# Mixer's first phase in a new order of copies, and weight splits placed anew at stage borders, in a two-block fp32 layer

## The chip, the cores and the metric
One core of a Trainium2 chip. The metric is the device time of one execution in microseconds (us), the median of several. Five engines share an on-chip memory (SBUF) and the accumulator banks (PSUM, eight banks `PS[0..7]` of 128 partitions by 2 KB): TensorE (PE, matrix products; PEld in the profile are its weight loads), VectorE (DVE), ScalarE (ACT), GpSimd (POOL) and SyncE (SP, which issues the transfers). Each engine runs its own list of instructions in order, and they wait for each other by semaphores.

## The reference
One activation matrix `x` (256 tokens by 1024, fp32) goes through two blocks. Cut to what matters:

```python
# first block
x = x + 0.5 * swiglu(rms_norm(x, ffn1_norm), w_gate, w_up, w_down)      # ffn1, inner width 2816
p = rms_norm(x, mix_norm) @ w_in                                         # mixer
p_rw = p_rw + (token_shift(p_rw) - p_rw) * mu_shift
p_r, p_k, p_v, p_w, p_a, p_g = split(p_rw)
for t in tokens:                                                         # per head, state 64 x 64
    sa = state @ (-kk[t])
    state = state * w[t] + outer(sa, kk[t] * a[t]) + outer(v[t], k[t])
    y[t] = state @ r[t]
y_rw = (group_norm(y) + bonus(r, k, v)) * g
y_pool = windowed_mean_minus_token(p_pool, windows=(2, 4, 8, 16)) @ w_pool * pool_scale
x = x + concatenate([y_rw, y_pool]) @ w_out
x = x + 0.5 * swiglu(rms_norm(x, ffn2_norm), ...)                        # ffn2, inner width 2816
x = rms_norm(x, final_norm)
# second block
x = x + concatenate([sliding_window_attention, differential_attention]) @ w_out_2
x = x + cross_attention(rms_norm(x, g_cross), rms_norm(mem, g_mem), w_cq, w_ckv, w_co)
x = x + square(relu(rms_norm(x, g_mlp) @ w_up)) @ w_down                 # mlp, inner width 4096
return rms_norm(x, g_final)
```

## The kernel before, in words
The whole kernel is one program per engine, ordered by hand; there is no planner. **Weights** come in units of 512 KB (128 x 1024 fp32). For every unit SP issues a load into one of three raw buffers (`load`, L382) once the unit before in that buffer is split. ACT rounds it to a high half `whi` (`split_hi`, L1110), DVE takes the difference to a low half `wlo` (`split_lo`, L1542), and PE makes three products of high and low halves for each tile (`mm`, L468; `a_unit`, `b_unit`, `b_half`). `whi` and `wlo` are rings of six; splits run four units ahead of PE (LEAD). The units are numbered through: ffn1 66, w_in 18 (`B_WIN`), w_out 8 (`B_WOUT`), ffn2 66, w_ckv 16, w_in2 18, w_out2 8, w_cq 8, w_co 8, mlp 64. The loops call `split_to(n)`, which brings the splits up to unit n, so the place of the call in an engine's list decides what stands behind a split.

**Norms.** ACT squares and sums x (`norm_sums`, L1123 table load, L1131, L1133), DVE makes the row factors (`norm_scale`, `norm_in_place` L1561), PE transposes x into PSUM (`norm_t`, L556), ACT writes the rounded high half of the transposed x (`norm_hi`, L1146), DVE the rest (`norm_lo`, L1587). The row factors go through a PE product and an ACT copy (`row_scale`, L1139) and are multiplied in later. `update_x` (L1609, L1611) adds a stage's output to x.

**ffn** (used twice): 22 chunks of gate unit, up unit, down unit. For a chunk ACT and DVE (`chunk`) copy the gate's and up's low parts (L1170, L1175), add, multiply by the row factors, take Silu (L1179), and make H, high half on ACT (L1183), low half on DVE (L1685). Three splits stand in each chunk: one ahead of the gate copy, one ahead of the up copy, one behind H. In ffn1's last chunk the third is left out. Ahead of chunk 0 both engines wait for the row factors.

**Mixer.** 18 w_in units; during them token shift, decays and the gates are made on all engines. Then the recurrence is computed by chunks of 128 tokens, four pairs of heads f: `products` of AA and K2 with KK into PSUM (16 matmuls a pair); on DVE `strict` masks them (L1851, both banks of a pair 128 x 512), adds the identity (L1855) and makes the first factor of an inverse (L1861, two); PE's `first`, and `outward` (products with PR); ACT copies first products (L1282) and the outward ones (L1288). Five rounds of `corrections` (PE), `corrected` (DVE, L1871) and merged products (PE) with `merged` copies (ACT, L1294, in the last round L1296, L1298) square the inverse. `causal` masks the outward products (L1879). In round k=2, 3, 4 DVE also makes pooling's window sums and means (L1826, L1842) and the bias. After round five come the pooling products, `t6` and `y12` products with their copies (L1308, L1312, L1316), the residual, and then W_out's halves (`fill_in`) filled in between the steps of the state. All rounds are laid out round by round: both pairs of f in corrections, then both in merged products. The splits of w_out units are made on ACT behind round one and on DVE behind `corrected(1, 1)` (`split_to(B_WOUT + RING)`); the squares of kk are summed with the squares as the moving operand, 8 rows by 256.

**Second block, memory projection** (`attention`, w_ckv): behind ffn2 PE transposes the memory; the norms of x for the two stages that follow (`norm_sums(4)` and `(5)`, `norm_in_place(4)`, `norm_scale(5)`) are put ahead of unit 0 and behind unit 2. PE's `norm_t("mem")` comes behind its wait for the last H (L591). **mlp**: 32 chunks of an up and a down unit (L2134); a chunk has one split ahead of its copies (`next_split(0)`) and one behind H (L1486, L1490 on ACT, L2154 on DVE).

Of the kernel before, what the change touches and what calls it, by code (L numbers as in the profile page):

```python
# [11 lines left out]
ACT = mybir.ActivationFunctionType  # L12
# [107 lines left out]
def build(nc, t, out):  # L120

    ctx = ExitStack()
    with ctx:
# [95 lines left out]
        MXR = MX[0:8, 0, :]  # L219

# [64 lines left out]
        def sems(names):  # L285
# [29 lines left out]
            sems("lk_mm y_first x1_mm x1_ev mm_mm mm_ev mm_ready t_mm t_ev xy_mm xy_ev yf_ev yf_zero")  # L315
        t6_mm, t6_ev, y12_mm, y12_ev, s_r_mm, s_r_ev, s_u_mm, s_u_ev, s_y_mm, s_y_ev, s_s_mm, s_s_ev = \
# [53 lines left out]
        N_MIXED = NF + NT  # L370
        PAIRS = ((0, 2), (1, 3))
# [94 lines left out]
        def _(pe):  # L466
# [76 lines left out]
            def norm_t(name):  # L543

                src = MEMX if name == "mem" else X
                for h in range(2):
                    for tt in range(NT):
# [6 lines left out]
                        for b in (2 * h, 2 * h + 1):  # L554
                            for c in (2 * b, 2 * b + 1):
                                last = pe.transpose(PS[4 + b][:, (c % 2) * T + tt * P:(c % 2) * T + (tt + 1) * P],  # L556
                                                    src[:, tt, c * P:(c + 1) * P], ident)
# [37 lines left out]
            def mix():  # L595
# [13 lines left out]
                for i in range(N_WIN):  # L609
# [9 lines left out]
                    if i == 12:  # L619
                        pe.wait_ge(sa_done, NF - 1)  # L620
                        pe.wait_ge(sq_ready, NF)
                        for f in range(NF):
                            last = mm(PS[6][0:8, 0:T], heads(f), SQ[:, f, :], start=(f == 0), stop=(f == NF - 1))
                        last.then_inc(ssq_mm, 1)
                    if i == 15:
# [5 lines left out]
                        for k in range(2):  # L631
                            mm(PS[6 + k][:, :], con("blk"), DP[:, 2 * k:2 * k + 2, :]).then_inc(bp_mm, 1)

# [9 lines left out]
                pe.wait_ge(w_mix, 14)  # L643
                pe.wait_ge(w_sum, N_WIN)
                pe.wait_ge(kk_ready, 2)
                lk = ((AA, KK), (K2, KK))
                products(0, lk, lk_mm)
                for c in range(NT):
                    for f in range(NF):
                        last = pe.transpose(PS[2 + c][:, f * P:(f + 1) * P], PV[:, f, c * P:(c + 1) * P], ident)  # L650
                    last.then_inc(tok_mm, 1)
                products(2, lk, lk_mm)
                pe.wait_ge(bon_done, 2)
                for k, src in enumerate((AA, K2)):
                    for f in range(NF):
                        last = pe.transpose(PS[6 + k][:, f * P:(f + 1) * P], src[:, f, 0:P], ident)
                    last.then_inc(tok_mm, 1)
                pe.wait_ge(tok_ev, 2)
                products(1, lk, lk_mm)
                pe.wait_ge(tok_ev, 4)  # L660
                products(3, lk, lk_mm)

                def first(n):

                    f = F_ORDER[n]
                    pe.wait_ge(y_first, n + 1)
                    for m in range(4):
# [5 lines left out]
                def outward(n):  # L673
# [3 lines left out]
                    pe.wait_ge(pr_ready, 1)  # L677
# [34 lines left out]
                for p in range(2):  # L712
                    for i in range(2):
                        first(2 * p + i)
                    for i in range(2):
                        outward(2 * p + i)
                    corrections(1, p)
                for k in range(1, 6):
                    if k > 1:
                        for p in range(2):  # L720
                            corrections(k, p)
                    for p in range(2):
                        merged(k, p)
                for g in range(NF):
                    pe.wait_ge(pooled, g + 1)
                    last = mm(PS[2 * (g // 2)][:, (g % 2) * T:(g % 2 + 1) * T], WPL[:, g, :], window(g, PAD))
                    if g % 2:
                        last.then_inc(pool_mm, 1)
                pe.wait_ge(xy_ev, 20)
                for f in range(NF):  # L730
                    for m in range(4):
                        ms = slice(64 * m, 64 * m + 64)
                        last = mm(PS[4 + 2 * (f // 2)][BOTTOM, (f % 2) * T + 64 * m:(f % 2) * T + 64 * m + 64],
                                  ULK[TOP, f, m // 2, m % 2, BOTTOM], XY[TOP, f, ms])
                    if f % 2:
                        last.then_inc(t6_mm, 1)
                pe.wait_ge(yf_ev, 4)
                for f in range(NF):
                    if f % 2 == 0:
                        pe.wait_ge(t6_ev, f // 2 + 1)  # L740
                    for m in range(4):
                        ms = slice(64 * m, 64 * m + 64)
                        last = mm(PS[1 + 2 * (f // 2)][TOP, (f % 2) * T + 64 * m:(f % 2) * T + 64 * m + 64],
                                  TP[BOTTOM, f, ms], yf(f, m)[BOTTOM, BOTTOM])
                    if f % 2:
                        last.then_inc(y12_mm, 1)
# [12 lines left out]

                def vt(c, f, hh):  # L760

# [1508 lines left out]
```

## Time and profile before
| | us |
|---|---|
| median of 3 runs (1012.08 to 1014.1) | 1013.05 |
| the profiled execution | 1011.99 |
| its span, first to last instruction | 1010.2 |
| PE busy | 956.7 (95%) |
| DVE busy | 664.6 (66%) |
| ACT busy | 538.5 (53%) |
| mean granted clock of PE (1 is full speed) | 0.987 |

Busy times are sums of instruction durations on an engine. A wait in the trace names the instruction that ended it, as "L468 <- DVE L1871": PE's line 468 stood idle until DVE's line 1871 released it. The profile names tiles by what they are in the program; `arena` is the large scratch area that the mixer's tiles are cut from.

### The profile page before, as it was taken

To read this page: it belongs to the slowest core of one execution; us is meant where nothing else is said; L and a number is where in the kernel's file an instruction comes from. 1 tells how busy PE (TensorE), PEld (TensorE's weight loads), DVE (VectorE), ACT (ScalarE), POOL (GpSimd) and SP (SyncE) were. 2 spreads that over 40 slices of the span, in tenths; PEclk is the share of its full clock that TensorE was granted. 3 is DMA by queue.
4 is the path that set the end of the run, shared out by engine and by line. 5 is a ranking of instruction groups with operands and counts; after the bars stand their busy time and mean duration, and the time that the engine had idled before them with its cause. 6 is when DMAs were issued, how large, how long until landed. Compare 5 with 4: busy or idle time off the path is not lost.

```text
span 1010.2 us, 17639 instructions
## 1 busy us (share of the span) xinstructions
PE 956.7 (95%) x6218; PEld 820.1 (81%) x6218; DVE 664.6 (66%) x1097; ACT 538.5 (53%) x967; POOL 29.9 (3%) x59
## 2 busy tenths in 40 slices
PE   6999999999969998999999998998899999999997
PEld 5888888889858877888888787887888877888885
DVE  4776766668947256776667775887456366666664
ACT  5655555586433336655555676536746446545452
POOL 3002000000000001000000000002100000000000
PEclk9999999999999999999999999997999999999999
DMA  6777666645301025766666656553037146666661
GB/s 192 225 220 220 189 188 188 183 135 135 129 5 41 1 84 126 218 192 187 189 186 199 193 154 180 147 167 105 1 109 222 45 128 185 206 185 190 187 203 47
DMA packets 204176, 153.61 MB, mean 152 GB/s; under 512 B 5323, under 2 KB 189872, under 8 KB 204128
## 3 DMA queue, kind: packets, MB, share of 16 engines
q1 hardware_dynamic: 202896, 151.08, 50.3%
q0 software_dynamic: 1232, 1.87, 0.9%
q8 instruction: 31, 0.51, 0.2%
q14 instruction: 17, 0.14, 0.0%
HBM read 151.89 MB, written 1.05 MB: 151 GB/s over the span
## 4 chain that ended last, share of the span: by engine, by line
PE 82%; DVE 7%; ACT 5%; DMA 3%; issue 2%; SPq 0%; DVEq 0%; ACTq 0%
PE ps L468 81%; DVE wlo L1542 2%; DMA raw<-in_w_ckv 2%; ACT whi L1110 2%; ACT arena L1131 1%; ACT XT L1146 1%; DVE XT L1587 1%; DMA raw<-in_ffn_w_gate 1%; DVE X L1561 0%; PE ps L556 0%; ACT arena L1288 0%; ACT arena L1294 0%; DVE arena L1851 0%; DMA raw<-in_w_down 0%; DVE X L1609 0%
## 5 line engine op out<-in xcount | busy, mean ns | idle before, releaser
L468 PE MATMUL ps<-XT,whi 128*128 128x512 f32 (+1 forms) x1584 | 522.6, 382 | 8.2 <-DVE XT L1587 7.0
L1542 DVE TENSOR_TENSOR wlo<-raw,whi 128x1024 fp32r<-128x1024 f32 x280 | 337.2, 1222 | 121.9 <-ACT whi L1110 100.5
L468 PE MATMUL ps<-XT,wlo 128*128 128x256 f32 x1440 | 405.3, 281 | 0.0
L468 PEld LDWEIGHTS ps<-XT,whi 128*128 128x128 f32 x1584 | 289.9, 189 | 71.1 <-issue 6.6
L1110 ACT ACTIVATE whi<-raw 128x1024 fp32r<-128x1024 f32 x280 | 293.1, 1055 | 62.8 <-PE ps L468 22.8
L468 PEld LDWEIGHTS ps<-XT,wlo 128*128 128x128 f32 x1440 | 273.6, 190 | 3.2
L468 PE MATMUL ps<-whi,H 128*128 128x512 f32 x608 | 177.9, 393 | 3.2 <-issue 2.0
L468 PEld LDWEIGHTS ps<-whi,H 128*128 128x128 f32 x608 | 108.9, 188 | 27.1 <-issue 3.1
L468 PE MATMUL ps<-arena 64*64 64x64 f32 (+6 forms) x1576 | 101.4, 254 | 14.1 <-DVE arena L1871 3.3
L468 PEld LDWEIGHTS ps<-arena 64*64 64x64 f32 (+3 forms) x1576 | 93.0, 157 | 22.0 <-issue 6.3
L468 PE MATMUL ps<-wlo,H 128*128 128x512 f32 x304 | 95.6, 392 | 0.0
L468 PEld LDWEIGHTS ps<-wlo,H 128*128 128x128 f32 x304 | 57.1, 188 | 13.3
L468 PE MATMUL ps<-whi,XT 128*128 128x512 f32 x192 | 57.4, 407 | 0.3 <-DVE XT L1586 0.3
L1170 ACT ACTIVATE arena<-ps 128x256 f32<-128x256 f32 x44 | 16.7, 379 | 51.2 <-PE ps L468 51.2
L468 PEld LDWEIGHTS ps<-whi,XT 128*128 128x128 f32 x192 | 36.2, 192 | 9.5 <-issue 1.6
L1175 ACT ACTIVATE arena<-ps 128x256 f32<-128x256 f32 x44 | 16.7, 379 | 44.2 <-PE ps L468 44.2
L1183 ACT ACTIVATE H<-arena 128x256 fp32r<-128x256 f32 x44 | 18.4, 417 | 39.7 <-DVE arena L1682 39.7
L1211 ACT ACTIVATE arena<-ps 128x256 f32<-128x256 f32 x42 | 15.9, 379 | 43.0 <-PE ps L468 42.9
L1486 ACT ACTIVATE arena<-ps 128x256 f32<-128x256 f32 x32 | 12.2, 381 | 48.2 <-PE ps L468 48.2
L1685 DVE TENSOR_TENSOR H<-arena,H 128x256 fp32r<-128x256 f32 x44 | 18.7, 425 | 24.4 <-ACT H L1183 24.4
L1674 DVE TENSOR_TENSOR arena<-ps,arena 128x256 f32<-128x256 f32 x44 | 18.6, 422 | 23.7 <-ACT arena L1170 23.5
L1490 ACT ACTIVATE H<-arena 128x256 fp32r<-128x256 f32 x32 | 13.4, 418 | 37.2 <-DVE arena L2151 37.2
(247 smaller groups left out, 710.0 us busy)
## 6 DMA issues: line engine op xcount, KB each, us to landing
raw<-in_ffn_w_gate SPq DMA_DIRECT2D x44, 512.0 KB, 4.5
raw<-in_ffn_w_up SPq DMA_DIRECT2D x44, 512.0 KB, 3.8
raw<-in_ffn_w_down SPq DMA_DIRECT2D x44, 512.0 KB, 4.5
raw<-in_w_in SPq DMA_DIRECT2D x36, 512.0 KB, 3.9
raw<-in_w_up SPq DMA_DIRECT2D x32, 512.0 KB, 4.7
raw<-in_w_down SPq DMA_DIRECT2D x32, 512.0 KB, 3.5
raw<-in_w_out SPq DMA_DIRECT2D x16, 512.0 KB, 3.4
raw<-in_w_ckv SPq DMA_DIRECT2D x16, 512.0 KB, 4.6
```

Source lines behind the costliest of these rows:

```text
L468: return pe.matmul(o, st, mv, start=start, stop=stop, skip_group_check=True)
L1110: act.activation(whi[:, n % RING, :], raw[:, n % RAW, :], ACT.Copy).then_inc(hi_ready, 1)
L1131: act.activation(SQJ, src[:, tt, :], ACT.Square, accum_out=SS[:, tt:tt + 1]).then_inc(ss, 1)
L1170: act.activation(GL[:, q, :], PS[4 + q][:, T:2 * T], ACT.Copy).then_inc(g_low, 1)
L1175: act.activation(UL[:, q, :], PS[6 + q][:, T:2 * T], ACT.Copy).then_inc(u_low, 1)
L1183: act.activation(H[:, q, 0:T], HS[:, q, :], ACT.Copy).then_inc(h_hi, 1)
L1211: act.activation(dst[:, i % 2, :], bank[:, T:2 * T], ACT.Copy).then_inc(sem_low, 1)
L1486: act.activation(UL[:, q, :], PS[4 + q][:, T:2 * T], ACT.Copy).then_inc(r_low, 1)
L1490: act.activation(H[:, q, 0:T], HS[:, q, :], ACT.Copy).then_inc(r_hi, 1)
L1542: dve.tensor_tensor(wlo[:, n % RING, :], raw[:, n % RAW, :], whi[:, n % RING, :].bitcast(F32), sub).then_inc(lo_ready, 1)
L1674: dve.tensor_tensor(GS[:, q, :], PS[4 + q][:, 0:T], GL[:, q, :], add).then_inc(g_raw, 1)
L1685: dve.tensor_tensor(H[:, q, T:2 * T], HS[:, q, :], H[:, q, 0:T].bitcast(F32), sub).then_inc(h_ready, 1)
```

## The change
Seven things, all on one core, with the same matrix products but for the turned squares:
1. **Start.** The first half of the first norm's sums stands ahead of the first splits; the other half behind a third split. In an ffn's chunk 0 the wait for the row factors and their copy stand inside the chunk, and a Silu of one column stands ahead, which loads its table.
2. **ffn's last chunk.** Its first two splits stand behind H, not ahead of the gate and up copies, on ACT and DVE.
3. **End of ffn2.** Half of the memory's transposes stand ahead of the wait for the last H, in other banks.
4. **Memory projection.** The norms' parts are spread over units 1, 3, 4, 5 and 8.
5. **w_in units.** The squares are summed with the squares as the stationary operand (16 matmuls, 8 columns each), clamped and inverted on 128 x 16, turned back by two transposes (unit 14) and copied by ACT (unit 15). KK's multiply is at unit 15, AA's norm multiplies and PR's at unit 16; V's transposes stand between units 16 and 17. Splits on DVE stop at `B_WOUT`, on ACT at `B_WOUT + RAW`.
6. **Products and rounds.** `strict` masks the left half of each bank; ACT copies the other half raw (`raw_keys`) and DVE masks it later in place (`strict_keys`). Products, first and outward are interleaved; rounds are interleaved over pairs and k: corrections(k,1), corrections(k+1,0), merged(k,1), merged(k+1,0). Window sums, means, bias, `causal`, pooling and the copies of `t6` and `y12` are placed anew; W_out splits on DVE are 1 behind `strict(3)`, 2 behind `corrected(1, 0)` and the rest at the end; on ACT one each behind rounds 3 and 4 and the rest at the end.
7. **mlp.** Both splits of a chunk stand behind H.

```diff
@@ PE
-            def norm_t(name):
+            def norm_t(name, halves=range(2)):
...
                 if f:
+                    norm_t("mem", [0])
                     pe.wait_ge(h_ready, 2 * FC)
-                    norm_t("mem")
+                    norm_t("mem", [1])
...
-                        for f in range(NF):
-                            last = mm(PS[6][0:8, 0:T], heads(f), SQ[:, f, :], start=(f == 0), stop=(f == NF - 1))
+                        for c in range(NT):
+                            for f in range(NF):
+                                last = mm(PS[6][:, 8 * c:8 * c + 8], SQ[:, f, c * P:(c + 1) * P], heads(f), start=(f == 0),
+                                          stop=(f == NF - 1))
                         last.then_inc(ssq_mm, 1)
+                    if i == 14:
+                        pe.wait_ge(sg_done, NF - 1)
+                        pe.wait_ge(nrm_set, 1)
+                        for c in range(NT):
+                            last = pe.transpose(PS[7][0:8, c * P:(c + 1) * P], MXT[:, 8 * c:8 * c + 8], ident)
+                        last.then_inc(nrm_turn, 1)
...
+                pe.wait_ge(kk_ready, 2)
+                products(0, lk, lk_mm)
+                pe.wait_ge(w_sum, N_WIN)
+                products(2, lk, lk_mm)
+                to_tokens(0)
+                to_tokens(1)
+                first(0)
+                pe.wait_ge(tok_ev, 4)
+                products(1, lk, lk_mm)
+                pe.wait_ge(pr_ready, 1)
+                outward(0)
+                first(1)
+                pe.wait_ge(bon_done, 2)
+                products(3, lk, lk_mm)
+                outward(1)
+                first(2)
+                outward(2)
+                first(3)
+                corrections(1, 0)
+                outward(3)
+                merged(1, 0)
+                for k in range(1, 5):
+                    corrections(k, 1)
+                    corrections(k + 1, 0)
+                    merged(k, 1)
+                    merged(k + 1, 0)
+                corrections(5, 1)
+                pooling(0)
+                sixth(0)
+                merged(5, 1)
+                across(0)
+                pooling(1)
+                sixth(1)
+                residual(0)
+                across(1)
@@ ACT, chunk of an ffn
-                    next_split(0)
+                    if j < FC - 1:
+                        next_split(0)
...
+                    if j == 0:
+                        if f == 0:
+                            act.activation(SMALL[:, 356:357], con("eps"), ACT.Silu)
+                        row_scale(RRB_FFN, PS[0], RRB_N[("ffn1", "ffn2")[f]])
...
                     if j < FC - 1:
                         next_split(2)
+                    else:
+                        next_split(0)
+                        next_split(1)
+                if f:
+                    act.activation(SMALL[:, 357:358], con("eps"), ACT.Silu)
                 split_to(b + LEAD)
-                row_scale(RRB_FFN, PS[0], RRB_N[("ffn1", "ffn2")[f]])
@@ ACT, mixer
+                def raw_keys(n):
+                    f = F_ORDER[n]
+                    act.wait_ge(l_strict, n + 1)
+                    for hh in range(2):
+                        ins = act.activation(ULK[:, f, hh, 2:4, :], four(PS[2 * f + hh][:, :])[:, 2:4, :], ACT.Copy)
+                    ins.then_inc(k2_raw, 1)
...
+                to_tokens(0)
+                to_tokens(1)
+                raw_keys(0)
+                to_tokens(2)
+                to_tokens(3)
+                first(0)
+                raw_keys(1)
+                outer(0)
+                raw_keys(2)
+                first(1)
+                outer(1)
+                raw_keys(3)
+                first(2)
+                outer(2)
+                first(3)
+                outer(3)
+                merged(1, 0)
+                for k in range(1, 5):
+                    merged(k, 1)
+                    merged(k + 1, 0)
+                    if k >= 3:
+                        split_to(B_WOUT + 1 + k)
...
@@ ACT, mlp (on DVE the same)
-                    next_split(0)
                     act.wait_ge(unit_used, B_MLP + max(0, 2 * j - 1) + 1 + dn)
...
                     act.activation(H[:, q, 0:T], HS[:, q, :], ACT.Copy).then_inc(r_hi, 1)
+                    next_split(0)
                     next_split(1)
@@ DVE, mixer
-                        dve.tensor_tensor(ULK[:, f, hh, :, :], four(PS[2 * f + hh][:, :]), bc(con("lt"), 4),
-                                          mul).then_inc(own_dve, own.next())
+                        ins = dve.tensor_tensor(ULK[:, f, hh, 0:2, :], four(PS[2 * f + hh][:, :])[:, 0:2, :], bc(con("lt"), 2),
+                                                mul)
...
+                for n in range(4):
+                    strict(n)
+                split_to(B_WOUT + 1)
                 corrected(1, 0)
+                split_to(B_WOUT + 3)
+                for k in range(1, 5):
+                    corrected(k, 1)
+                    corrected(k + 1, 0)
+                    if k == 1:
+                        for g in range(4):
+                            window_sum(g)
+                    elif k == 2:
+                        for g in range(4):
+                            window_mean(g)
+                    elif k == 3:
...
+                        for n in range(3):
+                            strict_keys(n)
+                    else:
+                        strict_keys(3)
+                        causal(0)
+                        bottom(0)
+                corrected(5, 1)
+                pooling(0)
+                causal(1)
+                bottom(1)
+                pooling(1)
+                causal(2)
+                causal(3)
+                split_to(B_WOUT + RING)
@@ DVE, memory projection
-                norm_in_place(4)
...
-                    if i == 2:
+                    if i in (1, 3):
+                        norm_in_place(4, [i // 2])
+                    if i == 5:
                         norm_scale(5, nth=RRB_N["mix2"])
```

## Rows read from the trace of the kernel before
**Rows 1.** The page: span, and part 4, the chain of work that ended last, by engine.
```profile
span 1010.2 us, 17639 instructions
...
PE 82%; DVE 7%; ACT 5%; DMA 3%; issue 2%; SPq 0%; DVEq 0%; ACTq 0%
```
**Rows 2.** Waits of PE, whole span: total us, times, longest.
```profile
PE ps L468 <- DVE XT L1587: 7.0, 6, 2.3
PE ps L468 <- DVE arena L1861: 4.4, 2, 3.2
PE ps L468 <- DVE arena L1871: 3.3, 2, 2.8
...
PE ps L468 <- ACT arena L1288: 2.7, 2, 1.4
...
PE ps L468 <- issue: 2.0, 2, 1.1
PE ps L468 <- DVE arena L1801: 1.9, 1, 1.9
...
PE ps L556 <- DVE H L1685: 1.7, 1, 1.7
PE ps L468 <- ACT arena L1294: 1.4, 4, 0.4
PE ps L468 <- DVE H L2154: 1.3, 3, 0.8
PE ps L878 <- DVE arena L1980: 1.2, 1, 1.2
PE ps L468 <- DVE arena L1980: 1.0, 1, 1.0
```
**Rows 3.** Stretches: us, busy of PE, PEld, DVE, ACT, POOL, clock, DMA.
```profile
299.00:304.87 5.87, 2.75 (x87) 2.51 (x84) 4.45 (x6) 2.34 (x3) 0.00 (x0) 1.00 0.31 97
304.87:308.28 3.41, 2.92 (x58) 2.73 (x54) 3.41 (x7) 1.09 (x2) 0.00 (x0) 0.50 0.50 146
```
**Rows 4.** The page's part 5, the two splits: busy us, mean ns, idle before.
```profile
L1542 DVE TENSOR_TENSOR wlo<-raw,whi 128x1024 fp32r<-128x1024 f32 x280 | 337.2, 1222 | 121.9 <-ACT whi L1110 100.5
...
L1110 ACT ACTIVATE whi<-raw 128x1024 fp32r<-128x1024 f32 x280 | 293.1, 1055 | 62.8 <-PE ps L468 22.8
```
**Rows 5.** Groups of instructions of DVE, ACT and PE, 269 to 336.
```profile
L1871 DVE TENSOR_TENSOR arena<-ps,CON 128x256 f32<-128x256 f32 x20 | 7.5, 418 | 11.6 <-PE ps L468 11.6
...
L1851 DVE TENSOR_TENSOR arena<-ps,CON 128x512 f32<-128x512 f32 x8 | 5.1, 684 | 0.1
...
L1294 ACT ACTIVATE arena<-ps 128x512 f32<-128x512 f32 x16 | 8.7, 595 | 17.7 <-PE ps L468 17.7
...
L1282 ACT ACTIVATE arena<-ps 128x256 f32<-128x256 f32 x4 | 1.5, 384 | 8.7 <-PE ps L468 8.7
...
L656 PE MATMUL ps<-CON,arena 128*128 128x128 f32 x8 | 1.1, 280 | 0.0
```
**Rows 6.** PE in order of time: start, us, what, in brackets the idle before.
```profile
278.72 0.68 PE L468 MATMUL ps<-CON,arena 64*64 64x64 f32 x16
...
281.14 2.06 PE L468 MATMUL ps<-arena 64*128 64x128 f32 x32
284.55 1.15 PE L468 MATMUL ps<-arena 64*64 64x64 f32 x32 [1.36 <-ACT arena L1288]
```
**Rows 7.** ACT, then DVE, in order of time at the end of ffn1.
```profile
197.89 1.28 ACT L1123 ACT_TABLE_LOAD   x1
199.18 0.20 ACT L1123 ACTIVATE SMALL<-CON 128x1 f32<-128x1 f32 x1
...
197.97 0.42 DVE L1685 TENSOR_TENSOR H<-arena,H 128x256 fp32r<-128x256 f32 x1 [0.55 <-ACT H L1183]
...
199.74 2.76 DVE L1609 SCALAR_TENSOR_TENSOR X<-ps,SMALL,X 128x512 f32<-128x512 f32 x4 [0.54 <-PE ps L468]
```
**Rows 8.** The page's part 6, a load of the mlp: KB, us to landing.
```profile
raw<-in_w_up SPq DMA_DIRECT2D x32, 512.0 KB, 4.7
```

More of the change, by code:

```diff
@@ L541, in b_last @@
                 b_banks(n, act, 1, 1).then_inc(unit_used, 1)
-            def norm_t(name):
+            def norm_t(name, halves=range(2)):
                 src = MEMX if name == "mem" else X
-                for h in range(2):
+                banks = MEM_BANKS if name == "mem" else T_BANKS
+                for h in halves:
                     for tt in range(NT):
@@ L710, in merged @@
                     last.then_inc(xy_mm, 1)
[L712 to L746, printed above, removed]
+                def pooling(k):
+                    for g in (2 * k, 2 * k + 1):
+                        pe.wait_ge(pooled, g + 1)
+                        last = mm(PS[2 * k][:, (g % 2) * T:(g % 2 + 1) * T], WPL[:, g, :], window(g, PAD))
+                    last.then_inc(pool_mm, 1)
@@ new lines, in first, with outer, merged @@
+                def first(n):
+                    f = F_ORDER[n]
+                    act.wait_ge(x1_mm, n + 1)
+                    act.activation(XY[:, f, 0:T], PS[2 * f][:, 0:T], ACT.Copy).then_inc(x1_ev, 1)
+                def outer(n):
+                    f = F_ORDER[n]
+                    act.wait_ge(mm_mm, n + 1)
+                    for hh in range(2):
+                        act.activation(MM[:, f, hh, :, :], four(PS[2 * f + hh][:, :]), ACT.Copy).then_inc(mm_ev, 1)
+                def merged(k, p):
+                    act.wait_ge(xy_mm, 2 * (k - 1) + p + 1)
+                    for f in PAIRS[p]:
+                        if k < 5:
+                            act.activation(XY[:, f, :], PS[2 * f + 1][:, :], ACT.Copy).then_inc(xy_ev, 1)
+                        else:
+                            act.activation(YZ[f // 2][TOP, 4 * (f % 2):4 * (f % 2) + 4, TOP],
+                                           four(PS[2 * f + 1][TOP, T:2 * T]), ACT.Copy)
+                            act.activation(XY[TOP, f, 0:T], PS[2 * f + 1][TOP, 0:T], ACT.Copy).then_inc(xy_ev, 1)
@@ new lines, in rest_of, with across @@
+                def rest_of(c):
+                    act.wait_ge(s_r_mm, c + 1)
+                    act.activation(RU[c][:, 0, :], PS[4][:, :], ACT.Copy).then_inc(s_r_ev, 1)
+                def across(p):
+                    act.wait_ge(y12_mm, p + 1)
+                    for f in PAIRS[p]:
+                        ins = act.activation(YZ[f // 2][TOP, 4 * p:4 * p + 4, BOTTOM],
+                                             four(PS[1 + 2 * p][TOP, (f // 2) * T:(f // 2 + 1) * T]), ACT.Copy)
+                    ins.then_inc(y12_ev, 1)
@@ L1319, in outward @@
+                act.wait_ge(bias_ready, 1)
+                for f in range(NF):
+                    ins = act.activation(GG[:, f, :], GG[:, f, :], ACT.Copy, scale=vec("ln_w", f))
+                ins.then_inc(gain_ready, 1)
+                pooling(0)
+                sixth(0)
+                merged(5, 1)
+                across(0)
+                pooling(1)
+                sixth(1)
+                rest_of(0)
+                across(1)
+                split_to(B_WOUT + RING)
                 def outward(c):
@@ L1688, in chunk @@
                         next_split(2)
+                    else:
+                        next_split(0)
+                        next_split(1)
                 split_to(b + LEAD)
-                dve.wait_ge(rrb_ready, RRB_N[("ffn1", "ffn2")[f]])
                 chunk(0)
```

259 lines of the change are left out of this document (127 added, 132 removed).

## The prediction
> **What bounds the kernel now.** I read the page first: TensorE (PE) is the engine of 82% of the chain that ended last, over a span of 1010.2 us [rows 1]. So the floor is PE's own work, and a change of order can only win what PE spends idle or at the low clock. Second the waits of PE [rows 2], which say what that idle time is made of. Five lines of them lie in the mixer's first phase, between its last w_in units and the first half of W_out, and nowhere else: the norm multiply L1801 1.9, the first masks L1861 4.4, the outward copies L1288 2.7, the corrections L1871 3.3, the merged copies L1294 1.4. That is 13.7 us, the only place where much is lost. The rest is in small pieces at borders: XT L1587 7.0 over six norms, H L1685 1.7 at the end of ffn2, two waits of 2.0 together that no semaphore explains (ahead of the first H of each ffn), 1.2 and 1.0 behind L1980 in the memory projection, 1.3 behind H L2154 in the mlp. Third the stretches of the clock [rows 3]: in 299 to 304.87 PE was busy 2.75 of 5.87 us, and then the granted clock is 0.50 for 3.41 us, in which PE is busy 2.92. At half speed about half of that is lost: 1.45 us.
>
> **The change part by part.** Split prices: 1.22 us on DVE, 1.06 on ACT for one unit [rows 4].
>
> *Mixer, products to W_out.* What makes PE wait before: `strict` on DVE masks the whole of two banks (2 x 0.68, L1851), adds the identity (0.68, as the L1851 price for equal size) and makes two first masks (2 x 0.42, by L1871 with as many elements to a partition) [rows 5]: 2.9 us for each of four pairs, while PE's own work between two firsts is shorter; outward products wait for copies; and two splits of 1.22 stand ahead of a correction (the 2.8 of L1871). The change masks only the left half there (2 x 0.42, by L1871, which is of that very shape and also reads PSUM), so a strict costs 0.84 + 0.68 + 0.84 = 2.4. The other half is copied raw by ACT (2 x 0.38, by L1282 of 256 elements, 0.77 together) and masked later on DVE (4 x 0.68), under corrections.
> I lay the new order out with PE's prices: a group of 16 products 1.03 (half of the 32 in 2.06), a first 0.68, a correction 1.15 [rows 6], eight transposes 1.1 (L656) [rows 5]. With 0 at the end of products(0): strict ends at 2.4, 4.8, 7.1, 9.5. PE has products(2) and tokens to 2.2, first(0) to 3.1, products(1), outward(0) to 5.2, first(1) to 5.9, products(3) to 7.1. DVE is thus no longer late by more than 0.2. Next late is ACT: behind outward(0) it has outer(0) 1.2, raw keys(2) 0.8, first(1) 0.4, so outward(1) starts at about 7.6 (0.5 idle); behind outward(1) outer(1) 1.2, raw keys(3) 0.8, first(2) 0.4, against PE's first(2) 0.68, so outward(2) waits 1.7. That is 2.3. The merged copies keep four waits of 0.35 (the 1.4 of L1294 now), and across(0) waits about 0.5 for its copies. Idle after: about 4.3 with 0.1 for first(0). The norm wait L1801 (1.9) goes: its multiplies and the V transposes now lie under the last two w_in units; what covers them is PE's own work on those units; uncovered they would be 2 x 0.68. The squares turned round: 16 matmuls with 8 columns for 4 with 256, and 2 transposes on PE; by 1.15 / 32 and 1.1 / 8 for each [rows 5, 6] this adds 0.85 and takes off some 0.4; I take 0.5. On DVE two small operations replace two larger ones, hidden before too. The low clock falls away as no stretch is left with PE idle half the time: 1.45. Splits moved out of the chain: DVE's one (1.22) behind strict(3) and two behind corrected(1,0) each cover under PE's 1.03 + 1.9, since PE's next need, corrected(1,1), comes after merged(1,0). The last three run after causal(3), before the first solve: PE there has W_out halves to fill in, for which three units are split.
> Sum: -13.7 + 4.3 + 0.5 - 1.45 = **-10.3**. Bounds: -5 (ACT's waits and the four corrections double) and -12 (ACT's copies cost PE nothing).
>
> *Border ffn1 to mixer.* Chunk 21 puts two splits behind H instead of ahead of its copies. That saves nothing, as those copies waited for PE. What it costs [rows 7]: before, DVE ends H at 198.39, copies VEC and begins the update of x at 199.74; ACT loads a table at 197.89. Now ACT has 2 x 1.06 to about 200.0 first; DVE's second split can't start before, ends at 201.3, VEC's small copy at about 201.6: update_x 1.9 later, with norm, XT and PE's first unit behind it. ACT's table load (1.28) is pushed too, but ends at 201.3, before the updated x is there. **+1.9**. Bounds 0 (DVE's update was waiting for PE's last unit, and part of it can hide) and +3.5 (a low-clock stretch as well).
> The profile has the table load at 197.89 with 1.28 us and the next activation at 199.18 [rows 7]: nothing between. The Trainium skill, page "ScalarE: Activation LUTs", section "What ACT_TABLE_LOAD costs", states about 2.66 us for a switch, of which some 1.38 is a drain; the trace disagrees and it decides. By the page the border would cost 1.4 more, about 1000.8 in all.
>
> *Start.* The first norm's sums ahead of a split, the row scale moved into chunk 0. Only H(0)'s wait (1.1, the longest of the two without releaser) can shrink, and the loads are next to be late: **-0.4**, bounds -1.2 and 0.
>
> *ffn2 start.* The same wait is 0.9 here (2.0 less 1.1). Silu's table is loaded ahead and row scale stands inside chunk 0: **-0.9**, bounds -0.9 and 0.
>
> *End of ffn2, memory projection.* Half the memory's transposes stand ahead of the wait for H, which hides the 1.7 of L1685 but for 0.2; the sums and in-place norms of `mem` and x are spread over units 1, 3, 4, 5 so that splits are not held up: of 1.2 + 1.0 at L1980 I take 1.6, since the weights' loads must catch up. The two splits behind H push only the border's own work, which here needs no table. **-3.1**, bounds -1.5 and -3.9.
>
> *mlp.* Both splits behind H, 32 chunks. The H chain gets shorter by one split each, so of L2154's 1.3 about 0.4 stays (the first chunks fill up): **-0.9**, bounds 0 and -1.3. Cover: a unit's split now runs after H, with PE holding units in a lead of four.
>
> Whole sum: -10.3 + 1.9 - 0.4 - 0.9 - 3.1 - 0.9 = **-13.7 us**. The profiled execution took 1011.99 and would take 998.3; the median of the three runs is 1.06 above that: 1013.05 - 13.7 = **999.4**.
>
> **Rivals.**
> 1. *ACT becomes the bound of the mixer.* Between products(0) and merged(1,0) it has 4 raw copies, 4 firsts, 8 outward, 2 tokens: 3.1 + 1.5 + 4.8 + 1.2 = 10.6 us against 15 of PE in my schedule. For: every outward now needs two of ACT's copies in turn and one late copy shifts the chain. Against: it had idle time in the phase. It keeps half of 10.3: 1004.6.
> 2. *The clock falls at the ffn1 border.* PE's idle grows by 1.9 there, and a fall cost 1.45 at 304.87 after a stretch of little work [rows 3]. With that, and the mixer's own low stretch kept: 999.4 + 1.6 + 1.5 = 1002.5. Against: the idle of the mixer that came before the fall was longer, 3.1 us within 5.87. The Trainium skill, page "TensorE: Matmul & The Clock Gate", Part 1, has the gate fall to half after an idle stretch; by that rule the rival holds if the border's idle is long enough, and the trace agrees in the mixer.
> 3. *The border costs nothing* as the update waits for the last unit anyway: 997.5.
> 4. *Slower: the mlp loop.* Both splits stand behind H in every chunk, so a raw slot comes free later and two loads follow each other. A w_up load takes 4.7 from issue to landing [rows 8], and by my count there are some 4 us before the unit is needed. From (13.7 + 2.0) / 32 = 0.49 us lost in each chunk the kernel is slower; at 0.6 it would be 1018.6. Against: PE hardly waits in that loop now (1.3 in three waits), and two splits (2.4) fit a chunk.
> 5. *The order doesn't take effect*, since the semaphores still tie the stages: 1013.
>
> **How the numbers follow.** Forecast 0.56, ACT 0.20, clock 0.10, border free 0.08, mlp 0.03, no effect 0.03. The range goes from 996 (border free and the mixer near its bound) to 1006 (ACT, and a low stretch). A measurement of this kernel can tell about 0.2%, 2 us. Faster 0.94, within 0.03, slower 0.03.
>
> **What would show it.** In the changed profile: mixer, PE's waits on L1861's and L1871's successors under 1 us together, on the ACT copies 3 to 4; strict's masks 0.42 each; no 0.50 clock between the products and W_out; first W_out half 10 us sooner after the last w_in unit. Border: PE's wait for XT between the last transposes and the first w_in unit no longer than before, but the transposes 1.9 later behind the last ffn1 unit. ffn2's end: no wait over 0.3 before the transposes. mlp: waits on H's second half under 0.5 in all. Wrong if the mixer's idle stays above 8, or if waits on wlo appear in the loops.

## The result and the profile after
The changed kernel takes 994.8 us (median of 4 runs, 993.62 to 995.92), the kernel before in the same runs 1013.47 (4 runs, 1012.08 to 1014.1): a ratio of 0.9822, 95% interval 0.9804 to 0.9839. I had forecast 999.4 with a range of 996 to 1006. The direction was right, but the gain is 18.7 us by the medians where I had 13.7, and the result lies 1.2 us below the range.

| | before | after |
|---|---|---|
| profiled execution, us | 1011.99 | 995.92 |
| its span | 1010.2 | 994.0 |
| PE busy | 956.7 | 952.2 |
| ACT busy | 538.5 | 541.2 |
| mean granted clock | 0.987 | 0.989 |

The page of the changed kernel, its span and chain (as [rows 1]):
```profile
span 994.0 us, 17685 instructions
...
PE 84%; DVE 7%; ACT 5%; issue 2%; DMA 2%; SPq 0%; DVEq 0%; ACTq 0%
```
PE's waits over its whole span (as [rows 2]: total, times, longest):
```profile
PE ps L472 <- DVE XT L1697: 7.5, 7, 2.4
...
PE ps L472 <- issue: 2.5, 1, 2.5
...
PE ps L472 <- ACT arena L1344: 1.7, 2, 1.4
PE ps L472 <- ACT arena L1358: 1.4, 4, 0.3
PE ps L561 <- DVE X L1720: 1.1, 2, 0.6
...
PE ps L472 <- DVE arena L1983: 0.6, 1, 0.6
...
PE ps L472 <- ACT arena L1367: 0.5, 1, 0.5
PE ps L472 <- DVE H L2298: 0.3, 1, 0.3
```
L1344 is the copy of a first product, L1358 the merged copy, L1983 the first masks, L1367 the copy ahead of `across`. In the mixer these are 1.7 + 1.4 + 0.6 + 0.5 = 4.2 us, where the five lines of [rows 2] had 13.7. Gone altogether are the waits on `corrected`, on the outward copies and on the norm multiply, both behind L1980 in the memory projection, and the one of the memory's transposes on H. Two are longer: the one ahead of ffn1's H(0) (2.5 for 1.1), and a new one on the update of x (L1720, 1.1).

Where the time went, stage by stage, as differences of PE's starts at the same instruction in the two traces:

| stage | forecast | first two traces |
|---|---|---|
| start, to ffn1's H(0) | -0.4 | +0.3 |
| border ffn1 to mixer | +1.9 | +1.55 |
| mixer, to the first W_out half | -10.3 | -8.75 |
| W_out to ffn2's norm | 0 | -1.6 |
| ffn2, to its H(0) | -0.9 | -1.0 |
| ffn2's end and memory projection | -3.1 | -3.6 |
| attention and cross | 0 | -1.8 |
| mlp | -0.9 | -1.4 |
| sum (of the unrounded) | -13.7 | -16.2 |

The border is as forecast in its kind. ACT, then DVE, in order of time in the changed kernel (as [rows 7]):
```profile
198.11 2.00 ACT L1149 ACTIVATE whi<-raw 128x1024 fp32r<-128x1024 f32 x2
200.12 1.28 ACT L1162 ACT_TABLE_LOAD   x1
201.41 0.20 ACT L1162 ACTIVATE SMALL<-CON 128x1 f32<-128x1 f32 x1
...
199.18 2.36 DVE L1652 TENSOR_TENSOR wlo<-raw,whi 128x1024 fp32r<-128x1024 f32 x2 [0.45 <-PE ps L472]
201.46 0.25 DVE L1827 COPY VEC<-ps 128x95 f32<-128x95 f32 x1
201.63 2.72 DVE L1720 SCALAR_TENSOR_TENSOR X<-ps,SMALL,X 128x512 f32<-128x512 f32 x4
```
The two splits stand ahead of the update, which begins at 201.63 for 199.74 [rows 7]. The table load is again 1.28 with the next activation right behind it.

Of the rest, much is the clock. Between two traces a stretch of half clock makes 1.6 to 2.0 us: the -1.6 behind W_out and the -2.0 in cross are two stretches (369.7 and 786.1 us before) that the changed kernel's trace doesn't have, and its mixer has one of its own. Stretches of the changed kernel, columns as in [rows 3]:
```profile
265.80:269.20 3.40, 3.40 (x9) 1.85 (x8) 0.00 (x1) 0.00 (x0) 0.00 (x0) 0.53 0.00 0
...
330.00:380.00 50.00, 47.12 (x306) 37.79 (x305) 26.74 (x43) 19.06 (x33) 3.19 (x6) 1.00 0.37 101
740.00:806.00 66.00, 63.44 (x336) 54.57 (x334) 35.87 (x60) 34.62 (x66) 0.00 (x0) 1.00 0.43 128
```
So one trace of each doesn't tell what the change brings. That became the main question.

By line, the 9.4 us of waits gone from the mixer aren't all of one kind. The norm multiply's 1.9 went with the new places of the multiplies and V's transposes. The longest wait on a correction stands behind two weight splits in DVE's list, which the change moves. PE, then DVE, before:
```profile
303.51 2.57 PE L468 MATMUL ps<-arena 64*64 64x64 f32 x64 [2.77 <-DVE arena L1871]
...
300.42 2.36 DVE L1542 TENSOR_TENSOR wlo<-raw,whi 128x1024 fp32r<-128x1024 f32 x2 [5.04 <-ACT whi L1110]
302.70 0.75 DVE L1871 TENSOR_TENSOR arena<-ps,CON 128x256 f32<-128x256 f32 x2
```
That leaves some 5 us for first masks, copies and the short wait on corrections, 9.0 before and 4.2 after. This division is read from who ended each wait; no run separates these parts.

### The profile page after: what moved, and what is told of

Same layout as the page of the kernel before. It is cut to its first block, busy times and chain, and to the rows that moved or that the text cites. A ratio compares the mean times of both kernels' runs of the same rounds, so it can differ in the third digit from the quotient of the medians.

```text
span 994.0 us, 17685 instructions
## 1 busy us (share of the span) xinstructions
PE 952.2 (96%) x6228; PEld 817.2 (82%) x6228; DVE 664.2 (67%) x1101; ACT 541.2 (54%) x980; POOL 30.0 (3%) x59
## 4 chain that ended last, share of the span: by engine, by line
PE 84%; DVE 7%; ACT 5%; issue 2%; DMA 2%; SPq 0%; DVEq 0%; ACTq 0%
PE ps L472 83%; DVE wlo L1652 2%; ACT whi L1149 1%; DMA raw<-in_w_ckv 1%; DMA raw<-in_ffn_w_gate 1%; DVE XT L1697 1%; ACT XT L1186 0%; DMA raw<-in_w_up 0%; ACT arena L1358 0%; DVE X L1720 0%; ACT arena L1170 0%; DVE arena L1889 0%; PE ps L561 0%; DVE arena L1844 0%; ACT arena L1351 0%
## 5 line engine op out<-in xcount | busy, mean ns | idle before, releaser
L1800 DVE TENSOR_TENSOR H<-arena,H 128x256 fp32r<-128x256 f32 x44 | 18.7, 426 | 24.4 <-ACT H L1229 24.4
```

Of the source, the lines that this page charges most:

```text
L1800: dve.tensor_tensor(H[:, q, T:2 * T], HS[:, q, :], H[:, q, 0:T].bitcast(F32), sub).then_inc(h_ready, 1)
```

## The experiments
**Do the parts add up?** `e1` is the kernel before with the changed mixer alone, `e2` the changed kernel with the mixer of before.
```diff
 # e1: kernel before
-            def mix():   # PE, ACT, DVE, as before
+            def mix():   # PE, ACT, DVE, as changed
 # e2: changed kernel, the other way round
```


> The kernel before with the mixer of the changed one (parts 5 and 6), nothing else. Theory of terms: PE's idle between the first product and the first W_out half falls from 13.7 to about 4.3 us as in the changed kernel, so the time falls by 9.4 us, and by up to 1.6 more for each 3.4 us stretch of half clock that is gone: 1002.5 to 1004, spans compared at equal clock 9.4 shorter. Rival (the gain is one of the clock): more than 12 us, with a granted clock of 0.991 or above against 0.987.

> The changed kernel with the mixer of before (parts 1 to 4 and 7 alone). Theory of terms: from the traces these parts are worth +0.3 (start), +1.5 (ffn1's border), -1.0 (ffn2's start), -3.6 (end of ffn2 and memory projection), -1.4 (mlp): together -4.2, so about 1009.2. With e1 the sum should be -14 to -18.5; if the two sum to less than 12 the parts need each other. Rival: the part of the gain beyond my forecast (another 2.5 in the profiled executions) is the clock's, and sits in neither kernel as a fixed place: then the half-clock stretches near 370 and 786 us come and go in both.

`e1`: 1002.01 us (before 1011.62, ratio 0.99, interval 0.9884 to 0.9915). `e2`: 1008.49 (ratio 0.9965, 0.995 to 0.9981). By the medians the two make 9.6 + 3.1 = 12.7, less than the 14 to 18.5 that I expected and less than the whole change (18.7 above, 15.0 in e5 below); by the spans of the single traces 11.2 + 4.9 = 16.1, as the whole change in the first traces (16.2). The waits of PE in e1's mixer are those of the changed kernel (here L1330, L1344, L1959, L1353):
```profile
PE ps L471 <- ACT arena L1330: 1.7, 2, 1.4
PE ps L471 <- ACT arena L1344: 1.4, 4, 0.3
PE ps L471 <- DVE arena L1959: 0.6, 1, 0.6
PE ps L471 <- ACT arena L1353: 0.5, 1, 0.5
```
So each part works without the other, but that they add up is shown by the spans alone. One place of loss shows in e1's trace: from the memory projection's first unit to W_out's in the second block it takes 154.9 us, where three traces of the kernel before have 151.5 to 152.5. A half-clock stretch at 595.9 is in it, PE's wait at the memory's norm is 2.4 for 1.2 before, and there is a wait of 1.1 on a low half. With one trace it stays open whether the faster mixer causes this. My expectation for e1, a fall of 9.4, fits by the median, which is 0.5 below the 1002.5 to 1004 given; e2 came 0.7 below 1009.2. But e2's trace had something new: in its mixer, the old one, the clock is half for some 10 us, from 290 to 300:
```profile
282.00:289.00 7.00, 4.28 (x96) 3.92 (x96) 4.54 (x10) 2.83 (x6) 0.00 (x0) 1.00 0.01 2
289.00:300.00 11.00, 7.58 (x100) 7.20 (x102) 2.71 (x6) 2.56 (x5) 0.98 (x2) 0.56 0.01 1
```

**The border and the mlp loop, each undone in the changed kernel.**
```diff
 # e3, on ACT and DVE
-                    if j < FC - 1:
+                    if j < FC - 1 or f == 0:
                         next_split(0)          # and the same for next_split(1)
...
-                    else:
+                    elif f:
                         next_split(0)
 # e4: mlp() of ACT and DVE as before
```


> The changed kernel, but in ffn1's last chunk the first two splits stand ahead of the gate and up copies again, as before (ffn2's last chunk as changed). My step says the two splits behind H push the update of x: +1.9 forecast, 1.5 seen between the two traces. Theory: 1.5 us faster than the changed kernel, PE's three waits around the transposes of the mixer's norm fall from 0.48 + 0.60 + 1.12 to 1.05 alone. Rival: the splits then stand in the way of the last chunk's copies and H comes later by as much, no difference within 0.3.

> The changed kernel with the mlp loop of before (one split ahead of the copies, one behind H). Theory: 0.9 to 1.4 us slower than the changed kernel, with three waits on L2154's like of 1.3 us in all back at the loop's start. Rival: a wait in every chunk too short to be listed (under 0.1) was also taken away, or the clumped loads cost something that the waits do not show: then the difference is outside 0.9 to 1.4.

`e3`: 993.46 us (ratio 0.9828, 0.9812 to 0.9844), `e4`: 997.64 (0.9865, 0.9846 to 0.9883). The changed kernel wasn't timed beside them: it is 994.8 above and 996.63 in e5 below, on another chip than e3 and e4. The intervals overlap, so steps of 1.5 us are read from the traces. In e3's trace the time from ffn1's H(0) to the first w_in unit is that of before within 0.1, 1.54 less than in the changed kernel: the step holds. In e4's the mlp is that of before within 0.1, 1.4 more than changed, and the waits on H in it are back whole:
```profile
PE ps L472 <- DVE H L2299: 1.3, 3, 0.7
```

**The changed kernel again, and three mends.** `e5` is unaltered. `e6`:
```diff
 # (a) as e3
 # (b) chunk of an ffn, ACT
                     act.activation(GL[:, q, :], PS[4 + q][:, T:2 * T], ACT.Copy).then_inc(g_low, 1)
+                    if j == 0:
+                        if f == 0:
+                            act.activation(SMALL[:, 356:357], con("eps"), ACT.Silu)
+                        row_scale(RRB_FFN, PS[0], RRB_N[("ffn1", "ffn2")[f]])
                     if j < FC - 1:
                         next_split(1)
-                    if j == 0:
-                        ...
 # (c) mixer, ACT; the same with raw_keys(3) and first(2)
-                raw_keys(2)
                 first(1)
+                raw_keys(2)
```


> The changed kernel again, unaltered, as the one to compare with on this chip. Theory: the places of the half-clock stretches before 680 us differ from the first trace (there one at 265.8), the waits of PE don't; the spans of two executions differ by about 1.5 us for each such stretch. Rival: the stretch at 265.8 belongs to the changed order and is there again.

> Three mends of the changed kernel: (a) ffn1's last chunk as before; (b) in chunk 0 Silu's table and the row scale stand ahead of the second split, where ACT sits waiting for a load; (c) in the products ACT makes first(1) ahead of raw keys(2), and first(2) ahead of raw keys(3). Theory: (a) 1.5; (b) the wait ahead of H(0), 2.5, goes, and DVE's split no longer stands between the row scale and the sum: 2.4; (c) the two waits on the copies of the firsts, 0.3 and 1.4, fall to about 0.0 and 0.6: 1.0. In all 4.9 us, 989 to 990. Rival to (b): ACT's copies are held by the load of the fifth unit whatever the order: 2.5 less gain. Rival to (c): first(3) then waits for raw keys(3) instead, no gain.

`e5`: 996.63 us, ratio 0.9851 (0.9827 to 0.9874). `e6`: 991.33, ratio 0.9787 (0.9762 to 0.9812), 5.3 less than e5 on the same chip; I expected 4.9, and 989 to 990 in all. The stretch at 265.8 isn't there in e5; the rival falls. (b) shows why the start had gained nothing. ACT, then DVE, of the changed kernel in order of time:
```profile
22.07 1.06 ACT L1149 ACTIVATE whi<-raw 128x1024 fp32r<-128x1024 f32 x1 [1.65 <-DMA raw<-in_ffn_w_gate]
23.15 1.28 ACT L1216 ACT_TABLE_LOAD   x1
24.45 0.20 ACT L1216 ACTIVATE SMALL<-CON 128x1 f32<-128x1 f32 x1
24.55 0.37 ACT L1178 ACTIVATE arena<-ps 128x256 f32<-128x256 f32 x1
...
25.02 0.43 DVE L1790 TENSOR_TENSOR arena<-arena 128x256 f32<-128x256 f32 x1 [3.28 <-ACT arena L1178]
25.37 1.22 DVE L1652 TENSOR_TENSOR wlo<-raw,whi 128x1024 fp32r<-128x1024 f32 x1
```
ACT sat 1.65 us waiting for a load, and only then loaded Silu's table and copied the row factors (L1178). DVE waited 3.28 for that copy, and its split, ready since 23.13, ran behind it. In e6:
```profile
21.39 1.28 ACT L1214 ACT_TABLE_LOAD   x1
22.68 0.20 ACT L1214 ACTIVATE SMALL<-CON 128x1 f32<-128x1 f32 x1
22.79 0.37 ACT L1178 ACTIVATE arena<-ps 128x256 f32<-128x256 f32 x1
23.05 1.05 ACT L1149 ACTIVATE whi<-raw 128x1024 fp32r<-128x1024 f32 x1
```
The wait ahead of H(0) is gone, and H(0) begins at 27.84 for 28.84 in e5. No half-clock stretch follows it, which is another 1.6 of the difference of these two traces; one at 357 in e6 takes as much back. (c): the waits on firsts in e6's mixer are 0.8 in one wait, for 1.7 in two:
```profile
PE ps L472 <- ACT arena L1344: 0.8, 1, 0.8
```

**What made the mixer's gain: the halved mask or the order?** `e7` masks whole banks again in the new order, `e8` makes ACT's raw copies dearer, `e11` puts the halved mask alone into the kernel before.
```diff
 # e7, changed kernel: DVE strict; raw_keys, strict_keys and their waits left out
-                        ins = dve.tensor_tensor(ULK[:, f, hh, 0:2, :], four(PS[2 * f + hh][:, :])[:, 0:2, :], bc(con("lt"), 2),
+                        ins = dve.tensor_tensor(ULK[:, f, hh, :, :], four(PS[2 * f + hh][:, :]), bc(con("lt"), 4),
 # e8, changed kernel: ACT raw_keys
-                        ins = act.activation(ULK[:, f, hh, 2:4, :], four(PS[2 * f + hh][:, :])[:, 2:4, :], ACT.Copy)
+                        for m in range(4):
+                            h = slice(64 * (m % 2), 64 * (m % 2) + 64)
+                            ins = act.activation(ULK[:, f, hh, 2 + m // 2, h], PS[2 * f + hh][:, T + 64 * m:T + 64 * m + 64], ACT.Copy)
 # e11, kernel before: strict, raw_keys, strict_keys as changed; on ACT raw_keys(0), raw_keys(1)
 # ahead of first(0), raw_keys(2), raw_keys(3) behind outer(0), outer(1); order of PE as before
```


> The changed kernel, but strict masks both halves of the banks again (two operations of 512 elements), with no raw copies on ACT and no later masking. It tells what the halved mask is worth in the new order. Theory (DVE was the bound of the products, so the half mask was needed): each strict is 0.52 longer, four of them 2.1; the waits on the first masks come back by about 2 us, the waits on ACT's firsts fall by about 1: 1 to 1.5 us slower than the changed kernel. Rival (the interleaving alone made the gain, ACT is the bound): ACT is relieved of 3.1 us and the kernel is not slower, or faster by 1.

> The changed kernel with each raw copy of 256 elements made in four of 64 on ACT: some 1 us more for each pair, 4 in all, and nothing else. Theory (ACT is next late in the products, as in my forecast): outward(1) and outward(2) wait about 1 us longer each, first(3) perhaps as well: 2 to 3 us slower. Rival (the slack on ACT is larger than the schedule says): under 0.5 us.

> The kernel before with the halved strict masks alone (raw copies on ACT, later masking on DVE in rounds 3 and 4), the order of products and rounds as before. With e7 it tells what the mask is worth without the order. Theory (after e7: the order made the gain, the mask only 0.4 in it): a strict is 0.52 shorter, of the 4.4 of waits on first masks about 1.5 go, so 1 to 2 us faster than before. Rival (my forecast's reading, DVE's length of strict is the cause): more than 3 us, with the waits on first masks under 1.

`e7`: 995.64 us (ratio 0.9843, 0.9818 to 0.9869), within the noise of e5. PE's waits in its mixer (L1976 first masks, L1341 copies of firsts, L1364 ahead of `across`):
```profile
PE ps L472 <- DVE arena L1976: 2.4, 4, 1.2
PE ps L472 <- ACT arena L1355: 1.4, 4, 0.4
PE ps L472 <- ACT arena L1341: 0.5, 1, 0.5
PE ps L472 <- ACT arena L1364: 0.5, 1, 0.5
```
DVE's waits rise by 1.8, ACT's fall by 1.2: the mixer is 0.4 us longer in the trace. Both of my theories had a true half; the mask is worth 0.4 in the trace and nothing that the times can tell, not the 1 to 1.5 expected.

`e8`: 998.04 us (0.9856, 0.9831 to 0.9881). The pieces cost less than I wrote (the group on ACT is 4.2 us busy for 2.6, so 1.6 more, not 4), and the waits on firsts grow by 0.8, to 2.5:
```profile
PE ps L472 <- ACT arena L1347: 2.5, 2, 1.8
```
Half of what is laid on ACT reaches PE; its trace also has the one half-clock stretch in a new mixer. By the medians it is 1.4 slower than e5, but the two intervals nearly coincide, so only the waits bear the direction of the theory; the expected 2 to 3 was out of a wrong price.

`e11`: 1013.2 us, ratio to before 1.0003 (0.9987 to 1.0018): nothing. Its waits (L1892 `corrected`, L1302 outward copies, L1882 first masks, L1817 norm):
```profile
PE ps L469 <- DVE arena L1892: 5.2, 4, 2.8
PE ps L469 <- ACT arena L1302: 3.2, 2, 1.9
PE ps L469 <- DVE arena L1882: 2.3, 1, 2.3
PE ps L469 <- DVE arena L1817: 1.9, 1, 1.9
```
The first masks fall from 4.4 to 2.3, as the theory said, but corrections and outward copies take it back (5.2 for 3.3, 3.2 for 2.7; corrections alone range from 2.8 to 4.2 in the traces of before). My reading is that in the old order PE comes earlier to the next wait of the same phase and nothing is ready for it; no run tests this. The mask without the new order gains nothing, and the new order without the mask keeps the gain (e7). So the gain is made by the new order together with the new places of the other operations; the mask only trims it.

**Does the clock belong to the order?** `e9` and `e10` are the kernel before, `e12` the changed kernel, unaltered, one trace each.

> The kernel before, unaltered, for a second trace. Question: do the half-clock stretches near 304, 370 and 786 us belong to its order, so that their absence is a gain of the change (3.6 us of the 16.2 between the first two traces lie at the last two)? Theory: they do not; each trace of a kernel has another set of single stretches before 680 us, and only those from about 690 to 720 and at the end are in every one. Rival: 304 and 370 stand behind the mixer's idle and are there again.

> The same once more, a third trace of the kernel before. Theory: PE's waits in the mixer are 13.7 us again within 0.1, the stretches elsewhere; rival: a stretch near 304 in each of the three.

> The changed kernel, unaltered, for a third trace. Theory: the waits of PE in the mixer 4.3 us as in both others, single half-clock stretches before 680 us at other places than 265.8 and 30; rival: a stretch at 265 to 269 again.

`e9`: 1012.63 us, `e10`: 1014.2, `e12`: 995.29. The waits of PE in the mixer are nearly the same in every trace of a kernel (13.1 to 14.5 in the old order, not within the 0.1 that I expected; 4.3 in the new). The clock isn't. e9 and then e10, the stretches of the mixer:
```profile
282.00:289.00 7.00, 4.28 (x96) 3.91 (x96) 4.53 (x10) 2.83 (x6) 0.00 (x0) 1.00 0.01 2
289.00:300.00 11.00, 7.49 (x98) 7.11 (x100) 2.72 (x6) 2.55 (x5) 0.98 (x2) 0.57 0.01 1
...
307.00:315.00 8.00, 6.06 (x122) 6.07 (x124) 8.00 (x15) 1.09 (x2) 0.00 (x0) 0.57 0.46 133
```
```profile
289.00:300.00 11.00, 8.80 (x133) 8.43 (x135) 1.59 (x4) 2.56 (x5) 0.98 (x2) 0.53 0.01 1
```
PE is busy 4.3 of 7 us, and then the clock is half for about 10 us, in e9 for another 7 at 307. The kernel before's first trace, the one I predicted from, had 3.4 us of it. Set side by side, the time from PE's first product with LWA (a small weight tile used among the w_in units; 220.6 in the first trace) to the first W_out half:

| mixer | trace | us | half clock between 270 and 330 |
|---|---|---|---|
| old | before | 115.1 | 3.4 |
| old | e2, e9, e10 | 118.4, 120.9, 118.4 | 10, 17 (and 3.4 at 263.2), 10 |
| old, half mask | e11 | 119.0 | 13 |
| new | after | 106.4 | none (3.4 at 265.8) |
| new | e1, e3, e4, e5, e12 | 104.9, 104.7, 104.7, 104.7, 104.7 | none |
| new, altered | e6, e7, e8 | 103.6, 105.2, 107.0 | none, none, 3.4 |

All five traces of the old order have it, in the new one only e8, whose ACT is slowed. So my theory in the expectation, that these stretches belong to no order, falls for the mixer; the rival, that 304 itself comes back, falls too: the place moves, but it is always within or behind the phase in which PE stands idle. When it comes isn't settled by the waits: the first trace had the same two longest waits on masks and outward copies, and kept the full clock until 304.9. So the link between idle time and low clock rests on how often they come together (five traces of five in the old order, one of nine in the new); no run changes the one alone. The theory holds for the single ones elsewhere: the stretch near 370 is in one of e2, e9, e10, e11 and in none of e5, e12; that near 786 in e10, not in e9; and one near 264 came in one trace of each order (e9 and after, 1.7 us). The stretch near 30 us is in e5 and again in e12, where I had expected another place. The first two made 3.6 us of the first traces' difference, and were luck.

The start has the reverse. Where the wait ahead of H(0) is 2.5 to 2.9 us, three of six traces have half clock behind it, as e5 and e12:
```profile
28.00:34.00 6.00, 5.16 (x17) 4.18 (x18) 5.16 (x8) 4.12 (x7) 0.00 (x0) 0.72 0.68 195
...
28.00:34.00 6.00, 5.49 (x19) 4.46 (x20) 5.43 (x8) 3.81 (x7) 0.00 (x0) 0.72 0.72 193
```
From H(0) to the mixer's norm these traces take 1.6 us more than the others of their kernel. With 1.1 to 1.7 us of wait (before, e1, e4, e7, e9, e10, e11) it is in none.

## Why the prediction was right and wrong
**Right: the schedule of the mixer.** Laid out from PE's and the copies' prices it gave 4.3 us of idle time; the traces have 4.25, and the single waits are at their places: 0.3 and 1.4 on ACT's firsts (0.5 and 1.7 forecast), 0.65 on DVE's (0.1), four of 0.35, 0.5 ahead of `across`. ACT was next late, as said. Against the trace of before the mixer falls by 10.4 (e3, e4, e5, e12) where I had 10.3.

**Wrong: the term of 1.45 for the low clock, and with it the -10.3 for the mixer.** I priced the one stretch of the one trace [rows 3] and took its absence for certain. The step was right in its sign, but the trace shown was the mildest: over the four traces of the old mixer unaltered (before, e2, e9, e10) it takes 117.8 us on average, with 1.7 taken off e9 for the stretch near 264: 13.1 more than the new one's 104.7, against my 10.3. The waits make 9.6 of that (13.9 on average, for 4.3), and by difference the low clock is worth some 3.5 us, or 4 with my 0.5 for the turned squares, where I had 1.45. The 2.8 us are the largest part of the 5.0 that the first comparison has beyond the sum, and more than the 1.2 by which it lies below the range, whose low end I had built from a free border and nothing of the clock. The times don't confirm it in full: e1, with the new mixer alone, gained 9.6 by the medians (8.6 to 11.7 by its interval), and e5's 15.0 is near my sum. The Trainium skill, page "TensorE: Matmul & The Clock Gate", Part 1, has idle halve the clock; I set that against the change, and in the mixer the traces agree with it, but there it works for the change. At the ffn1 border, where I had it as a rival, no trace shows it; at the start it does in three traces of six.

**Wrong: what in the mixer does it.** I named the length of `strict` as what makes PE wait and the halved mask as what takes it away. e7 and e11 show the mask to be worth 0.4 in the new order and nothing in the old. What is left is the order of products, firsts, outwards and rounds over the pairs, and the places of the norm multiplies, V's transposes and W_out's splits. By the waits the last three account for up to 1.9 + 2.8 = 4.7 us of the 9.4, the order for the rest, where a copy gets a product of another pair to hide under; this share is argued, not shown by a run.

**The border,** +1.9 forecast, 1.54 seen, and undone by e3: right. The bound that the update waits for PE's last unit (my rival 3) didn't hold.

**The start,** -0.4 forecast, +0.3 in the first two traces; over all of them H(0) begins at 28.3 us on average with the start of before (5 traces) and at 28.4 with the changed one (8 traces), so nothing was gained. I moved the row scale into chunk 0 and counted it as nothing, while ACT's list put it and Silu's table behind a split that waits for a load. The step "next to be late are the loads" was right, and it made the moved work late with them. The units ahead of it did come earlier, and the wait behind them took it back: 1.6 to 2.9 us for 1.1 to 1.7, with the low clock behind it in three traces.

**Too careful:** at the end of ffn2 and in the memory projection I took 3.1 of the 3.9 of waits; all went (4.1 in e5's trace, 3.6 in the first, both against the first trace of before). These waits vary too: e9 has 2.7 of them, and against it the stage gains 2.4 to 2.9. So the 3.1 may have been right. In the mlp 0.9 of 1.3; 1.4 went. A wait that is taken from one place didn't come back at the next in either stage.

**The base.** The execution I summed against was faster than all three timed runs beside it, and the medians of the same kernel moved between calls by 1 to 2 us (before 1011.62 to 1013.47, changed 994.8 and 996.63). The gain is 15.0 to 18.7 us by two comparisons whose intervals overlap; the range I gave misses the first and holds the second.

Not tried: each of the other placements in the mixer alone (squares turned round, V's transposes, the place of W_out's splits). No run divides the -10.4 among them but for the mask.

## What to carry to other kernels
Price a stretch of low clock from more than one trace, and from the idle time ahead of it: where PE stands idle for a large share of a phase, count on more low clock there than one trace shows, and on its going when the idle goes. Before an operation is shortened, look whether the order puts another chain's work under its wait; here the new order, with the operations moved along with it, took 9.4 us of waits, the shorter operation 0.4. When work is moved in an engine's list, ask which load the instruction ahead of it waits for: a table load and a 128 x 256 copy moved ahead of such a split, with two other swaps in order, gave 5.3 us more (e6, 991.33 us, the fastest version here).

## What the runs showed that I had not expected
The same program's half-clock time in the mixer was 3.4, 10 and 17 us in three traces, with PE's waits alike to 1.4 us (before, e10, e9), at a difference of up to 5.8 us in that phase, and the spans still lay within 2.2 us, since stretches elsewhere came and went against it. And a table load took 1.28 us with 0.02 ahead of it and the activation 0.01 behind it, at all places of both kernels but the program's first and one where the activation waited for DVE. So a one-column activation that loads the table is worth putting where its engine waits anyway.
